# High and low FFN input side by side in 512-column passes, on a two-layer encoder trunk kernel

## What is computed

```python
D_MODEL, SEQ, DEPTH, D_FF, CONV_WIDTH = 1024, 256, 2, 2816, 3

def conv_gated_mlp(h, w_up, conv_w, w_down):
    u = h @ w_up                                   # (256, 1024) @ (1024, 5632)
    up = jnp.pad(u, ((0, 0), (1, 1), (0, 0)))      # along the tokens
    u = sum(up[:, t:t + S] * conv_w[t] for t in range(CONV_WIDTH))
    gate, val = jnp.split(u, 2, axis=-1)
    return (jax.nn.gelu(gate, approximate=True) * val) @ w_down

for l in range(DEPTH):
    ...
    h = rms_norm(x, ffn_pre_norm[l])
    x = x + rms_norm(conv_gated_mlp(h, w_up[l], ffn_conv[l], w_down[l]), ffn_post_norm[l])
```

## Time and profile before

| | |
|---|---|
| median of 3 runs | 1049.89 us (1049.77 to 1050.1) |
| the profiled execution's own time | 1048.77 us |
| its span, from first to last instruction | 1046.8 us |
| TensorE (PE) busy | 1027.2 us, 98% |
| VectorE (DVE) busy | 656.3 us, 63% |
| ScalarE (ACT) busy | 587.2 us, 56% |
| from the first pass of U0 to the first of D10, first layer | 335.90 to 519.20 us |

### The profile page before, as it was taken

The page is one execution under the profiler, slowest core; times in us unless marked ns, Lnnn a source line. Parts: engine busy times, 40 slices in busy tenths (PEclk is TensorE's granted clock), DMA queues, the critical chain, the costliest instruction groups (busy, mean ns, idle before and its releaser), DMA issues.

```text
span 1046.8 us, 15963 instructions
## 1 busy us (share of the span) xinstructions
PE 1027.2 (98%) x6332; PEld 921.4 (88%) x6332; DVE 656.3 (63%) x866; ACT 587.2 (56%) x843; POOL 126.1 (12%) x233
## 2 busy tenths in 40 slices
PE   7999999999999999999999999999999999999997
PEld 7889999888877999999898899998888789999996
DVE  5535566655585776767674355666555767676765
ACT  5557666556446555454475666665553466455453
POOL 4352124000000000000024321230000000000000
PEclk9999999999999999999999999999999999999999
DMA  7655445444443655545355544564445445554541
GB/s 221 208 157 166 123 143 169 152 161 161 141 169 133 201 192 171 200 162 205 117 177 176 154 141 121 150 203 161 129 157 178 161 138 176 190 200 163 201 162 40
DMA packets 106221, 170.79 MB, mean 163 GB/s; under 512 B 3377, under 2 KB 72804, under 8 KB 106148
## 3 DMA queue, kind: packets, MB, share of 16 engines
q1 hardware_dynamic: 104860, 166.88, 48.3%
q10 hardware_dynamic: 1208, 2.63, 0.7%
q0 software_dynamic: 80, 0.26, 0.2%
HBM read 168.72 MB, written 1.05 MB: 162 GB/s over the span
## 4 chain that ended last, share of the span: by engine, by line
PE 91%; DVE 4%; ACT 2%; DVEq 2%; issue 1%; DMA 1%; POOL 0%; ACTq 0%; POOLq 0%
PE bank L1269 27%; PE bank L1271 26%; PE bank L1270 26%; PE bank L1559 2%; PE bank L1466 1%; PE bank L1487 1%; DVEq L1127 1%; PE bank L1552 1%; DVE merged L1128 1%; DVE hT_lo L997 1%; PE bank L1475 1%; PE bank L1503 1%; PE bank L1510 1%; PE bank L1549 1%; PE bank L1517 1%
## 5 line engine op out<-in xcount | busy, mean ns | idle before, releaser
L976 DVE TENSOR_TENSOR w_lo<-w_raw,w_hi 128x2048 fp32r<-128x2048 f32 (+3 forms) x174 | 362.9, 2098 | 191.0 <-ACT w_hi L648 190.9
L648 ACT ACTIVATE w_hi<-w_raw 128x2048 fp32r<-128x2048 f32 (+3 forms) x174 | 302.5, 1753 | 52.0 <-PE bank L1271 47.7
L1269 PE MATMUL bank<-w_hi,hT_lo 128*128 128x512 f32 (+2 forms) x700 | 258.3, 369 | 0.0
L1271 PE MATMUL bank<-w_hi,hT_hi 128*128 128x512 f32 (+2 forms) x700 | 253.1, 362 | 0.0
L1270 PE MATMUL bank<-w_lo,hT_hi 128*128 128x512 f32 (+2 forms) x700 | 252.7, 361 | 0.0
L1269 PE MATMUL bank<-hT_hi,w_lo 128*128 128x256 f32 x704 | 199.9, 284 | 3.4 <-DVE hT_lo L997 3.2
L1271 PE MATMUL bank<-hT_hi,w_hi 128*128 128x256 f32 x704 | 199.2, 283 | 0.0
L1270 PE MATMUL bank<-hT_lo,w_hi 128*128 128x256 f32 x704 | 199.2, 283 | 0.0
L1269 PEld LDWEIGHTS bank<-w_hi,hT_lo 128*128 128x128 f32 x700 | 131.8, 188 | 15.2 <-issue 2.0
L1271 PEld LDWEIGHTS bank<-w_hi,hT_hi 128*128 128x128 f32 x700 | 131.5, 188 | 14.1
L1270 PEld LDWEIGHTS bank<-w_lo,hT_hi 128*128 128x128 f32 x700 | 131.9, 188 | 13.0
(11 more groups left out here) (203 smaller groups left out, 1248.6 us busy)
## 6 DMA issues: line engine op xcount, KB each, us to landing
w_raw<-in_w_up_dram SPq DMA_DIRECT2D x44, 1024.0 KB, 4.9
w_raw<-in_w_in_dram SPq DMA_DIRECT2D x36, 1024.0 KB, 5.0
w_raw<-in_w_in_dram SPq DMA_DIRECT2D x36, 768.0 KB, 4.4
w_raw<-in_w_down_dram SPq DMA_DIRECT2D x22, 1024.0 KB, 5.2
w_raw<-in_w_out_dram SPq DMA_DIRECT2D x8, 1024.0 KB, 5.0
w_raw<-in_w_in_dram SPq DMA_DIRECT2D x8, 672.0 KB, 4.2
w_raw<-in_w_branch_mla_dram SPq DMA_DIRECT2D x4, 1024.0 KB, 4.9
w_raw<-in_w_branch_diff_dram SPq DMA_DIRECT2D x4, 1024.0 KB, 5.0
```

The lines of the kernel that those rows point to most:

```text
L648: nc.scalar.activation(w_hi[:, n % RING, 0:nk * cols], raw[:, n % RING, 0:nk * cols], ACT.Copy).then_inc(hi_done, 1)
L976: V.tensor_tensor(w_lo[:, n % RING, s], raw[:, n % RING, s], w_hi[:, n % RING, s].bitcast(F32), ALU.subtract).then_inc(lo_done, 1)
L1269: PE.matmul(dst, lhs[1], rhs_hi, start=start, stop=False)
L1271: return PE.matmul(dst, lhs[0], rhs_hi, start=False, stop=stop)
```

## The change

The high and the low input are put in one tensor, `hT[:, k, 0, :]` and `hT[:, k, 1, :]`, so that they lie side by side. An up block (j, k) now takes two passes: high weights with 512 moving columns (high and low input), and low weights with the 256 columns of the high input, added to the first half. Each channel block j gets a bank of its own: columns 0 to 255 hold high times high plus low times high, columns 256 to 511 hold high times low. An up piece takes two banks, and the four banks hold two up pieces instead of four. To add the two halves, ScalarE copies the second halves of both banks to `up_sum` and VectorE adds the first halves to it. The convolution then reads `up_sum`.

```diff
-        hT_hi = sb("hT_hi", [P, KD, SEQ], F32R)
-        hT_lo = sb("hT_lo", [P, KD, SEQ], F32R)
+        hT = sb("hT", [P, KD, 2, SEQ], F32R)
+        hT_hi, hT_lo = hT[:, :, 0, :], hT[:, :, 1, :]
...
+            up_sum = sb("up_sum", [P, 2, 2, SEQ], scope=four)
+        def up_banks(c):
+
+            return up_bank[:, 2 * (c % 2):2 * (c % 2) + 2, :]
...
                             act.wait_ge(piece_used, l * NPIECE + (RING + n + 1))
+                            if c >= 2:
+
+                                act.wait_ge(conv_done, BASE + l * 2 * NU + (c - 1))
+                            nc.scalar.activation(up_sum[:, c % 2, :, :], up_banks(c)[:, :, SEQ:2 * SEQ], ACT.Copy).then_inc(up_copied, 1)
+                            act.wait_ge(up_summed, l * 2 * NU + (c + 1))
...
                                 last = nc.scalar.activation(conv[:, u % 2, b, j * SEQ:(j + 1) * SEQ],
-                                                            bank[4 + c % 4][:, j * SEQ:(j + 1) * SEQ], ACT.Copy,
+                                                            up_sum[:, c % 2, j, :], ACT.Copy,
                                                             scale=par_all[:, l, 44 + ch:45 + ch])
...
+                            dve.wait_ge(up_copied, l * 2 * NU + (c + 1))
+                            V.tensor_tensor(up_sum[:, c % 2, :, :], up_sum[:, c % 2, :, :], up_banks(c)[:, :, 0:SEQ], ALU.add).then_inc(up_summed, 1)
+                            dve.drain()
                             dve.wait_ge(conv_mid, l * 2 * NU + (c + 1))
...
-                    if c >= 4:
-
-                        pe.wait_ge(conv_done, BASE + l * 2 * NU + (c - 3))
+                    if c >= 2:
+
+                        pe.wait_ge(up_summed, l * 2 * NU + (c - 1))
                     for j in range(2):
                         for k in range(8):
                             if j == 0:
                                 wait_turned(l, kind, c, k)
-                            last = passes(bank[4 + c % 4][:, j * SEQ:(j + 1) * SEQ],
-                                          (hi[:, k, j * P:(j + 1) * P], lo[:, k, j * P:(j + 1) * P]),
-                                          hT_hi[:, k, :], hT_lo[:, k, :], k == 0, k == 7)
+                            dst = up_banks(c)[:, j, :]
+                            PE.matmul(dst, hi[:, k, j * P:(j + 1) * P], hT[:, k, :, :].rearrange("p s q -> p (s q)"),
+                                      start=k == 0, stop=False, skip_group_check=True)
+                            last = PE.matmul(dst[:, 0:SEQ], lo[:, k, j * P:(j + 1) * P], hT_hi[:, k, :], start=False, stop=k == 7,
+                                             skip_group_check=True)
```

More of the change, by code:

```diff
@@ L354, in build_trunk @@
             par_rows = sb("par_rows", [44, 4 * DEPTH, P], scope=four)
-        bank = [ctx.enter_context(nc.psum_tensor(f"bank{i}", [P, 512], F32)) for i in range(8)]
+            up_sum = sb("up_sum", [P, 2, 2, SEQ], scope=four)
+        bank = [ctx.enter_context(nc.psum_tensor(f"bank{i}", [P, 512], F32)) for i in range(4)]
+        up_bank = ctx.enter_context(nc.psum_tensor("up_bank", [P, 4, 512], F32))
+        bank += [up_bank[:, i, :] for i in range(4)]
         S_BANK, O_BANK = (bank[4], bank[5]), bank[7]
@@ L401, in build_trunk @@
         post_squares, x_ready = sem("post_squares"), sem("x_ready")
-        conv_mid, conv_done = sem("conv_mid"), sem("conv_done")
+        up_copied, up_summed, conv_mid, conv_done = sem("up_copied"), sem("up_summed"), sem("conv_mid"), sem("conv_done")
         gelu_done, g_ready, g_hi_done, g_lo_done = sem("gelu_done"), sem("g_ready"), sem("g_hi_done"), sem("g_lo_done")
@@ L1217, in _ @@
                                 o = j * SEQ
-                                cv, src = conv[:, u % 2, b, :], bank[4 + c % 4]
+                                cv, src = conv[:, u % 2, b, :], up_sum[:, c % 2, :, :].rearrange("p j q -> p (j q)")
                                 V.scalar_tensor_tensor(out=cv[:, o + 1:o + SEQ], in0=src[:, o:o + SEQ - 1], scalar=par_all[:, l, ch:ch + 1],
```

## The result

The changed kernel takes 1069.17 us (median of 4 runs, 1068.16 to 1071.39) against 1049.83 us (4 runs, 1049.47 to 1050.1). The ratio is 1.0192, 95% interval 1.0178 to 1.0206: 19 to 20 us slower. The forecast was 1064.7 with a range of 1057 to 1073.

What follows compares the result with a forecast made beforehand. TensorE bounds now, 16.98 us a round; VectorE and ScalarE by turns grow from 13.99 by 3.28 to 17.27 and take over. Losing 7.4 us a layer, 14.8 for two, gives 1063.6, plus 1.1 to the median: 1064.7, range 1057 to 1073.

Steps and rivals of the forecast that it cites:

- TensorE is relieved and loses its place as the bound: FFN rounds: TensorE's round falls from 16.98 to 16.6 us, below the 17.27 of VectorE and ScalarE working by turns.
- The string of 13.99 us: VectorE and ScalarE work by turns (taps, product, splits), counted per round without waits for TensorE; forecast to reach 17.27 us.
- The sum: VectorE adds the two halves of each up piece, ahead of the taps: 0.68 us, twice a round.
- The turn: After each sum VectorE stands still while ScalarE makes the middle tap, handovers included: 0.96 us, twice a round.
- 10R - 165.33: Loss a layer in us, with R the round's length: 7.4 us at R = 17.27.
- Where TensorE waits: New TensorE waits a layer: about 3.6 us before U5, 0.7 eight times for `w_lo`, 3.3 before D10.
- rival 4: TensorE's clock falls in the new gaps before U5 and D10: 1066.5 to 1070 us, chance 12%.
- the case with 73%: The forecast as costed, VectorE and ScalarE by turns setting the pace, no clock loss: 1064.7 us, 73%.
- the forecast's own bounds: R between 16.8 and 17.8 us, loss between 5 and 25 us: 1058 to 1072 us.
- TensorE's saving of 0.012 us a block: Up blocks: three 256-column passes (0.360 us) become one of 512 and one of 256 (0.348), saving one pass start.
- a sign that it would be wrong: Up passes of 512 moving input columns running at another rate than the down pieces' 0.228 us.
- The taps' source: Taps reading SBUF instead of a bank: no change taken; rival with taps 65 ns shorter gave 1059 us, 5%.

Runs made afterwards that it cites:

- the run without the turn: Changed kernel, but the middle tap reads the banks' first halves right after the copy, without waiting for VectorE's sum: 1050.21 us, ratio 1.0007.
- the run with the clock kept up: Changed kernel with identity matmuls of no other use in TensorE's long gaps, 28 before U5 and 30 before D10 a layer: 1066.29 us, ratio 1.0165.
- the first two experiments without the string: Changed kernel without copy and sum: 1044.54 us; changed kernel with the middle tap reading banks, not waiting for the sum: 1050.21 us.

## Why the prediction was right, step by step

- **TensorE is relieved and loses its place as the bound**: right, shown by the old passes with the new sum (1069.87).
- **The string of 13.99 us grows by 3.28 to 17.27**: measured 17.36. The sum took the 0.68 us of the earlier trace rows. The turn took 0.98 instead of 0.96; ScalarE's pair 0.91 instead of 0.88. By the prediction's formula, 10R - 165.33, the measured round gives 8.3 us a layer, and 8.4 were measured.
- **The turn, in which VectorE only waits, is the larger of the two terms**: right, 0.98 us for the turn beside 0.68 for the sum. Filling one turn a round with a `w_lo` took 7 us off. What counts is a place on the string: a second copy on ScalarE, off it, costs 3 us, a second sum on VectorE, on it, 28. That the turns cost more than the sums is read from these lengths; the run without the turn does not show it.
- **Where TensorE waits**: right in place, and near in size. The predicted size is in brackets: 3.1 us recorded before U5 (3.6), 0.31 to 0.43 before the later ones (0.7, which is reckoned from pass starts and shortened by the slower passes), 3.0 before D10 (3.3). ScalarE's middle tap, which had waited for TensorE, now waits for VectorE's sum every time, 89.6 us in all 44 turns, as forecast.
- **The clock**, rival 4 at 12%: right in kind, and given far too little chance. It is not a rival to the forecast but comes on top of it, and the measured 1069.17 lies in the 1066.5 to 1070 that rival 4 was given. So the case that came was the one with 12%, and the case with 73%, the string without the clock, did not come by itself; the result lies in the range, and in the 1058 to 1072 of the forecast's own bounds, because both were wide enough to take in the clock's 2.9 us, which the sum left out. The gaps of 3.0 to 3.1 us were nearly as long as the one of 3.53 us behind which the clock had fallen, and it fell behind three of the four. In the run with the old passes it fell behind all four (0.62 to 0.72 in the 6 to 9 us from each), and with one `w_lo` moved behind a gap of 2.4 us before D10 too (0.79 from 524 to 532 us). The string alone gives 1049.83 + 16.8 = 1066.6, the run with the clock kept up 1066.29, and the clock the 2.9 us from there to the median. The Trainium skill, "TensorE: Matmul & The Clock Gate", section on HAM oscillation, warns of idle gaps between bursts of matmuls, and this trace agrees (0.50 behind the gap before the last D10). The warning should have moved more of the chance.
- **TensorE's saving of 0.012 us a block**: mis-sized, measured 0.007. The prediction had named another rate of the wide passes as a sign that it would be wrong; the sign came, 0.24 us instead of 0.228, and moved nothing, since the string was the bound. It put the expectations of the first two experiments without the string 3 to 4 us too low.
- **The taps' source**: the taps took 481 ns from SBUF (0.88 for a pair, 0.87 before). The Trainium skill, "VectorE: DVE Perf Modes", section on the TRN2 errata, has a smaller fixed cost from SBUF, 65 ns less by the estimate in the prediction. That does not show here: the same line took 478 ns from the bank.

The error is 4.5 us. The clock is 2.9 of it and the string's 0.09 us a round nearly 2, which is 0.4 more than there is to explain.

## What to carry to other kernels

Before you lighten the engine that is 98% busy, add up the string of the others without their waits for it: here it was 13.99 us under 16.98, so it had room for one sum and one turn a round (15.7 us) and not for two (17.3). An instruction that hands over to another engine and waits for the answer costs the queue behind it the whole answer time, so look for work that can stand in the hole, and give the new scheme only to as many pieces as the string has room for. And ask of each new gap on TensorE whether its clock survives it: here four gaps of 3.0 to 3.1 us cost some 3 us in all beside the waiting itself.

## What I had not expected of the hardware

The distance from a 512-column pass to the next depends on its neighbours. Among its like it is 0.227 us, between passes of 256 it is 0.24; in the same mixed order the passes of 256 keep their 0.12. Eight wide passes followed by eight narrow ones took 2.79 us, the same sixteen mixed 2.82. Why this is so was not tried.
